# Alternating five convolution chunks with the z chunks of a mixer, and computing the convolution's Silu from a tanh and a product

## The reference, cut to what matters

```python
proj = u @ w_in
z, xbc, dt_raw, u5, g_a, g_b = jnp.split(proj, SPLITS, axis=-1)
# ssd branch
xbc = jax.nn.silu(causal_depthwise_conv(xbc, conv_w, conv_b))   # width 3072, 4 taps
xs, bm, cm = xbc[:2048], xbc[2048:2560], xbc[2560:3072]         # (on the last axis)
dt = softplus(dt_raw + dt_bias); a = -exp(a_log)
y = ssd_chunked(xs * dt, a * dt, bm, cm) + d_skip * xs
y = y * silu(z)
y_a = groupnorm(y) @ w_branch_a
# s5 branch
y_b = s5_branch(u5, ...) @ w_branch_b
merged = sigmoid(g_a) * y_a + sigmoid(g_b) * y_b
```

## Time and profile before

| | |
|---|---|
| median of 3 runs | 3229.38 us |
| range of the runs | 3227.72 to 3231.2 us |
| the profiled execution | 3236.26 us |
| span in its profile | 3234.4 us |
| mean granted TensorE clock | 0.953 of full speed |
| PE / DVE / ACT busy | 92% / 69% / 52% of the span |

### The profile page before, as it was taken

One profiled execution on the slowest core, in us unless ns is written; L12 is line 12 of the kernel. 1 busy time (PEld: TensorE's weight loads), 2 busy tenths in 40 slices (PEclk: granted clock), 3 DMA queues, 4 the chain that ended last, 5 costly groups with the idle time before them and its releaser, 6 DMA issues.

```text
span 3234.4 us, 55445 instructions
## 1 busy us (share of the span) xinstructions
PE 2979.0 (92%) x22709; PEld 2763.9 (85%) x22709; DVE 2232.5 (69%) x2614; ACT 1674.7 (52%) x1838; POOL 74.2 (2%) x68
## 2 busy tenths in 40 slices
PE   8988899989989889898989988988779999999997
PEld 7988898979989888888889987988579989999996
DVE  5778975655556779857555554555568888888887
ACT  4444566334444454563344444443456666666665
POOL 0000003000000000030000000000000000000000
PEclk9998999999999988999999998999889999999998
DMA  7553342446545533433555553545089999999996
GB/s 233 165 157 104 94 133 90 157 141 199 178 157 178 175 105 93 131 106 118 170 167 177 181 170 112 187 156 183 1 288 310 318 343 342 319 318 337 347 319 212
DMA packets 485886, 619.87 MB, mean 192 GB/s; under 512 B 31841, under 2 KB 436211, under 8 KB 485747
## 3 DMA queue, kind: packets, MB, share of 16 engines
q1 hardware_dynamic: 485747, 617.90, 58.3%
HBM read 616.81 MB, written 1.05 MB: 191 GB/s over the span
## 4 chain that ended last, share of the span: by engine, by line
PE 77%; DVE 13%; ACT 5%; issue 3%; DMA 1%; DVEq 0%; SPq 0%; ACTq 0%
PE PS L602 12%; PE PS L603 12%; PE PS L604 12%; PE PS L655 11%; PE PS L882 5%; PE PS L884 5%; PE PS L883 5%; DVE w_lo L1575 3%; PE PS L1064 3%; PE PS L1065 2%; PE PS L1066 2%; ACT w_hi L1139 2%; ACT w_hi L1506 1%; PE PS L1076 1%; PE PS L784 1%
## 5 line engine op out<-in xcount | busy, mean ns | idle before, releaser
L602 PE MATMUL PS<-x_hi,w_hi 128*128 128x256 f32 x3360 | 976.7, 291 | 13.1 <-DVE x_lo L2042 7.1
L603 PE MATMUL PS<-x_hi,w_lo 128*128 128x256 f32 x3360 | 967.2, 288 | 0.0
L604 PE MATMUL PS<-x_lo,w_hi 128*128 128x256 f32 x3360 | 966.1, 288 | 0.0
L1575 DVE TENSOR_TENSOR w_lo<-raw,w_hi 128x2048 fp32r<-128x2048 f32 x313 | 711.6, 2288 | 333.6 <-ACT w_hi L1139 332.9
L1139 ACT ACTIVATE w_hi<-raw 128x2048 fp32r<-128x2048 f32 x313 | 598.5, 1913 | 398.3 <-PE PS L655 249.1
L602 PEld LDWEIGHTS PS<-x_hi,w_hi 128*128 128x128 f32 x3360 | 662.9, 197 | 24.7 <-issue 12.0
L603 PEld LDWEIGHTS PS<-x_hi,w_lo 128*128 128x128 f32 x3360 | 663.0, 197 | 1.9
L604 PEld LDWEIGHTS PS<-x_lo,w_hi 128*128 128x128 f32 x3360 | 661.7, 197 | 0.0
L882 PE MATMUL PS<-w_hi,x_hi 128*128 128x256 f32 x1488 | 429.6, 289 | 8.4 <-DVE x_lo L2225 6.7
L884 PE MATMUL PS<-w_lo,x_hi 128*128 128x256 f32 x1488 | 421.8, 283 | 0.0
L883 PE MATMUL PS<-w_hi,x_lo 128*128 128x256 f32 x1488 | 421.7, 283 | 0.0
(11 more groups left out here) (393 smaller groups left out, 4098.0 us busy)
## 6 DMA issues: line engine op xcount, KB each, us to landing
raw<-in_w_gu_moe_dram SPq DMA_DIRECT2D x98, 1024.0 KB, 8.5
XC<-in_w_gu_moe_dram SPq DMA_DIRECT2D x80, 1024.0 KB, 9.6
raw<-in_w_in_dram SPq DMA_DIRECT2D x64, 1024.0 KB, 5.8
raw<-in_w_down_moe_dram SPq DMA_DIRECT2D x48, 1024.0 KB, 8.6
raw<-in_ffn_w_gate_dram SPq DMA_DIRECT2D x44, 1024.0 KB, 5.4
raw<-in_ffn_w_up_dram SPq DMA_DIRECT2D x44, 1024.0 KB, 6.7
raw<-in_ffn_w_down_dram SPq DMA_DIRECT2D x44, 1024.0 KB, 5.0
G<-in_w_down_moe_dram SPq DMA_DIRECT2D x40, 1024.0 KB, 9.5
```

The source lines that it names most:

```text
L602: mm(dst, w_hi[:, slot, w0:w0 + P], hi, start=start, stop=False, skip_group_check=True)
L603: mm(dst, w_lo[:, slot, w0:w0 + P], hi, start=False, stop=False, skip_group_check=True)
L604: return mm(dst, w_hi[:, slot, w0:w0 + P], lo, start=False, stop=True, skip_group_check=True)
L1575: tt(w_lo[:, slot, :], raw[:, slot, :], w_hi[:, slot, :].bitcast(F32), SUB)\
```

## The change

Two things are changed in both layers.

The order of the ticks: x(13) to x(19) stay (channels 8 to 11, 0, 1, 2). From tick 20 on z and x alternate, z(0), x3, z(1), x4, z(2), x5, z(3), x6, z(4), x7, and the last three are z(5), z(6), z(7). The first z tick is k = 20 instead of 25, and the work that was hung on it moves with it. The buffers of z change, since `conv_out` is now in use for longer.

The Silu of the convolution: `prm` holds the convolution's weights and biases times 0.5, so `conv_out` holds half the sum, ACT takes Tanh of it in tick k+2, and a new DVE instruction at the head of tick k+2 (`conv_silu`) forms (tanh + 1) * conv_out. To halve these columns the copy to `prm` is split in two. ACT's last tap of x(k) now waits for DVE's product of x(k-2). In the alternating ticks ACT also waits, ahead of the eviction of an x chunk, for DVE's `gate_z` of the tick before.

```diff
-TICKS = ... + [("x", i) for i in CONV_ORDER] + [("z", i) for i in range(8)]
+TICKS = [("u", i) for i in range(4)] + [("d", 0)] + [("g", i) for i in range(8)] + [("x", i) for i in CONV_ORDER[:7]] \
+    + [tick for i in range(5) for tick in (("z", i), ("x", i + 3))] + [("z", i) for i in (5, 6, 7)]
...
-        zbuf = [conv_out[:, 0], conv_out[:, 1], act_out[:, :, :]]
+        zbuf = [act_out[:, :, :], stage[:, :, :], wk(6912, 2, T)]
...
-                    fn(prm[:, :], PS[:, 7, 0:192], ACT.Copy).then_inc(s["prm_ready"], n.one("prm_ready"))
+                    fn(prm[:, 0:72], PS[:, 7, 0:72], ACT.Copy)
+                    fn(prm[:, 72:192], PS[:, 7, 72:192], ACT.Copy, scale=0.5).then_inc(s["prm_ready"], n.one("prm_ready"))
...
                 if i not in CONV_ORDER[:2]:
-                    act.wait_ge(s["silu_conv"], n.last("silu_conv"))
+                    act.wait_ge(s["silu_conv"], n.due("silu_conv"))
...
-                fn(XC[:, 2 * i:2 * i + 2, :], conv_out[:, i % 2, :, :], ACT.Silu)\
-                    .then_inc(s["silu_conv"], n.one("silu_conv"))
+                fn(XC[:, 2 * i:2 * i + 2, :], conv_out[:, i % 2, :, :], ACT.Tanh)\
+                    .then_inc(s["conv_tanh"], n.one("conv_tanh"))
...
                     if kind == "x":
+                        if z_at(k, 1) is not None:
+                            act.wait_ge(s["c_evicted"], n.due("c_evicted", k - ticks_seen))
+                            ticks_seen = k
                         last_tap(i)
...
+            def conv_silu(i):
+
+                dve.wait_ge(s["conv_tanh"], n.due("conv_tanh"))
+                x = XC[:, 2 * i:2 * i + 2, :]
+                stt(x, x, 1.0, conv_out[:, i % 2, :, :], ADD, MULT).then_inc(s["silu_conv"], n.one("silu_conv"))
...
                 for k, (kind, i) in enumerate(TICKS):
+                    if conv_at(k, 2) is not None:
+                        conv_silu(conv_at(k, 2))
...
-                    if k == 25:
+                    if k == Z_AT[0]:
                         dve.wait_ge(s["dtok_psum"], n.due("dtok_psum"))
...
+                    if z_at(k, 1) is not None:
+                        ssd_inputs(z_at(k, 1))
                     if kind == "z":
-                        if i >= 1:
-                            ssd_inputs(i - 1)
                         gate_z(i)
-                        if i >= 2:
-                            ssd_outputs(i - 2)
+                    if z_at(k, 1):
+                        ssd_outputs(z_at(k, 1) - 1)
```

More of the change, by code:

```diff
@@ L56 @@
 MIX = FFN1 + 3 * STEPS
-C_Z = MIX + 25
-C_A = C_Z + 8
+C_A = MIX + 33
 C_G = C_A + 8
@@ L214, with conv_at, z_at @@
 CONV_ORDER = [8, 9, 10, 11, 0, 1, 2, 3, 4, 5, 6, 7]
-TICKS = [("u", i) for i in range(4)] + [("d", 0)] + [("g", i) for i in range(8)] + [("x", i) for i in CONV_ORDER] \
-    + [("z", i) for i in range(8)]
-CONV_AT = [kind for kind, _ in TICKS].index("x")
+TICKS = [("u", i) for i in range(4)] + [("d", 0)] + [("g", i) for i in range(8)] + [("x", i) for i in CONV_ORDER[:7]] \
+    + [tick for i in range(5) for tick in (("z", i), ("x", i + 3))] + [("z", i) for i in (5, 6, 7)]
+X_AT = [TICKS.index(("x", i)) for i in CONV_ORDER]
+Z_AT = [TICKS.index(("z", i)) for i in range(8)]
+def conv_at(k, behind):
+    return CONV_ORDER[X_AT.index(k - behind)] if k - behind in X_AT else None
+def z_at(k, behind=0):
+    return Z_AT.index(k - behind) if k - behind in Z_AT else None
 S5_TILES = S5_PAIRS // 4
@@ L366, in build @@
                  "picked gathered scattered scatter_turned scatter_ready hidden_ready hidden_turned kh_ready y_copied sum_added mean_sum "
-                 "z_tanh moe_silu gate_odd up_odd down_odd gate_ready up_ready down_ready gate_used up_used down_used "
+                 "z_tanh conv_tanh moe_silu gate_odd up_odd down_odd gate_ready up_ready down_ready gate_used up_used down_used "
                  "act_step dve_step pool_step pool_waited sp_waited out_sent").split()
@@ L819, in mixer @@
                             part(t)
-                    if MIX + k == C_Z - 1:
+                    if k == Z_AT[0] - 1:
                         pe.wait_ge(s["e_read"], n.due("e_read"))
@@ L1269, in last_tap, with conv_tanh @@
                        scale=prm[:, 168 + t:169 + t], bias=prm[:, 72 + t:73 + t])
-            def silu_conv(i):
+            def conv_tanh(i):
                 act.wait_ge(s["tap_done"], n.due("tap_done"))
@@ L1309, in mixer @@
                 run[0] = 0
+                ticks_seen = 0
                 for k, (kind, i) in enumerate(TICKS):
@@ L1319, in mixer @@
                             part(t)
[L1320 to L1323, removed]
+                    if conv_at(k, 2) is not None:
+                        conv_tanh(conv_at(k, 2))
+                    if z_at(k, 1) is not None:
+                        ssd_decay(z_at(k, 1))
                     if kind == "z" and i >= 3:
@@ L1341, in mixer @@
                     if kind == "z":
-                        if i < 2:
-                            act.wait_ge(s["silu_conv"], n.last("silu_conv"))
                         wait_used(pos[0] + 1)
@@ L1349, in mixer @@
                 ssd_decay(7)
+                n.due("c_evicted", 33 + 8 - ticks_seen)
+                n.due("silu_conv", 2)
                 n.due("y_psum", 4)
@@ L1845, in s5_local, with evicted @@
                 dve.wait_ge(s["local_ready"], n.last("local_ready"))
-            def taps(i):
[L1849 to L1853, removed]
+            ticks_seen = [0]
+            def evicted(k):
+                if k >= ticks_seen[0]:
+                    dve.wait_ge(s["c_evicted"], n.due("c_evicted", k + 1 - ticks_seen[0]))
+                    ticks_seen[0] = k + 1
+            def conv_silu(i):
+                dve.wait_ge(s["conv_tanh"], n.due("conv_tanh"))
+                x = XC[:, 2 * i:2 * i + 2, :]
+                stt(x, x, 1.0, conv_out[:, i % 2, :, :], ADD, MULT).then_inc(s["silu_conv"], n.one("silu_conv"))
+            def taps(i):
+                evicted(X_AT[CONV_ORDER.index(i)])
                 for j in range(3):
@@ L1898, in gate_z @@
                 z = zbuf[i % 3]
-                stt(z, z, 1.0, PS[:, 4 + (C_Z + i - MIX) % 2, :].rearrange("p (u n) -> p u n", u=2), ADD, MULT)\
+                stt(z, z, 1.0, PS[:, 4 + Z_AT[i] % 2, :].rearrange("p (u n) -> p u n", u=2), ADD, MULT)\
                     .then_inc(s["c_evicted"], n.one("c_evicted"))
             def ssd_outputs(i):
-                dve.wait_ge(s["c_evicted"], n.due("c_evicted"))
+                evicted(Z_AT[i])
                 for u in range(2):
@@ L1939, in mixer @@
                 for k, (kind, i) in enumerate(TICKS):
+                    if conv_at(k, 2) is not None:
+                        conv_silu(conv_at(k, 2))
                     if k == 5:
-                        dve.wait_ge(s["c_evicted"], n.due("c_evicted", 5))
+                        evicted(4)
                         stt(dt_rows[:, 1, :], dt_rows[:, 0, :], -1.0, dt_rows[:, 0, :], MULT, MIN)\
@@ L1959, in mixer @@
                         s5_scan(t)
-                    if 0 <= k - CONV_AT - 1 < 12:
-                        taps(CONV_ORDER[k - CONV_AT - 1])
-                    if k == 25:
+                    if conv_at(k, 1) is not None:
+                        taps(conv_at(k, 1))
+                    if k == Z_AT[0]:
                         dve.wait_ge(s["dtok_psum"], n.due("dtok_psum"))
@@ L1975, in mixer @@
                 ssd_outputs(7)
-                n.due("silu_conv", 2)
+                n.due("c_evicted", 33 - ticks_seen[0])
+                ticks_seen[0] = 0
                 for i in range(8):
```

## The result

The changed kernel took 3242.87 us, the median of 13 runs (3235.49 to 3246.12), and the kernel before 3231.14 us in as many runs beside it (3227.72 to 3234.66). The ratio is 1.0035, with an interval of 1.0027 to 1.0042, so it is 11.7 us slower. The forecast was 3233.6 us, 4.2 us slower than the median of the first three runs, in a range of 3228 to 3240.

What follows compares the result with a forecast made beforehand. PE was taken as the bound, except DVE in ticks 15 and 16. Per layer 1.22 + 0.61 + 0.25 = 2.08 us, 4.2 for two, on the median of 3229.4 gave 3233.6 us, range 3228 to 3240.

Steps and rivals of the forecast that it cites:

- what bounds what: First layer's mixer: DVE bounds ticks 15 and 16, PE the stretches 412.6 to 466.0 and 474.1 to 540.1 us.
- the 12.8 us of the table loads: Rival: ten removed ACT table loads of 1.28 us were on the path, making the kernel faster, 3220.8 us; chance 0.04.
- only stalls could be won or lost: PE is already full, so only the dt_tok stall could be won: 1.6 us and 1.7 us of lost clock per layer.
- the products of ticks 15 and 16: DVE bounds these ticks, so two added products of 0.61 us come on the path: 1.22 us a layer, up to 1.6.
- the sign that the prediction named: Sign of being right: PE's wait for the S5 result at L737's successor grows from 4.8 to about 5.4 to 6.0 us.
- ticks 18 and 19: ACT's last tap waits for DVE's product of two ticks before, but is just not late: 0, up to 0.5 us.
- The closed chain: Last tap, w_hi, w_lo, product, next last tap: 6.2 us against a 5.76 us tick; would slow long runs of x ticks.
- the price of tick 20: First z tick: the product lengthens PE's dt_tok wait from 1.60 to 2.21 us: +0.61, up to 0.8 + 0.5.
- A clock under 0.7 after the dt_tok stall: One of the signs listed in advance that would show the prediction wrong.
- The rival on the clock: After the longer wait at the first z tick the clock falls deeper: 2.5 us more per layer, 3238.6 us; chance 0.17.
- the term for prm: Both layers' heads: splitting the prm copy in two costs +0.25 us each, between 0.1 and 0.36.

Runs made afterwards that it cites:

- no_product: The changed kernel, new tick order and tanh on ACT, without DVE's product, so it computes something else: 3229.71 us, 0.9994 of the kernel before.
- before_again: The kernel before, unchanged, run for a second profile: 3230.46 us.
- silu_only: The changed kernel with the old order of ticks, keeping the tanh on ACT and the product on DVE: 3246.26 us, 1.0047 of the kernel before.
- before_copy_later2: The kernel before with two idle DVE products ahead of the dt_tok copy, lengthening that wait in each layer: 3238.58 us, 1.0022 of the kernel before.
- after_copy_first: The changed kernel with DVE's dt_tok copy moved to the head of the first z tick, ahead of product and taps: 3229.24 us, 0.9994 of the kernel before.
- after_again: The changed kernel, unchanged, run for a second profile: 3242.57 us.

## Why the prediction was wrong

**Right: what bounds what.** PE is full through the alternating ticks at a clock of 1.00, no engine falls behind there, and the 12.8 us of the table loads did not come (no_product). The trace of before also settles what the earlier trace rows left open, whether ACT stands still behind a load: one load of tick 19 runs from 427.26 to 428.54 us, and the Silu behind it starts at 428.55. The reading that only stalls could be won or lost held; what a stall costs beyond its own length is the step that failed, below.

**Right in kind, too large in size: the products of ticks 15 and 16.** The term was 1.22 us a layer. In the second layer the two kernels start the mixer alike, at 1129.8 and 1130.1 us, and PE comes out of the dt_tok stall 1352.4 - 1130.1 = 222.3 us later, against 1378.9 - 28.8 (five ticks of 5.76) - 1129.8 = 220.3 before. The shift is 2.0 us, and 1.3 of it is the longer wait for dt_tok, so 0.7 us are left for the products of ticks 15 and 16, little more than half of the term. In the first layer it can't be read. The wait at L748 grew by 0.6 us, the sign that the prediction named, but the other wait for an S5 result, L738 (the old L727), shrank from 3.4 to 1.0 us, and in before_again L737 had 3.2 us. PE came out of the stall 219.7 us after the start of the mixer, against 220.2 and 218.6 in the two profiles of before.

**Partly wrong: ticks 18 and 19, "It is just not late: 0, up to 0.5."** For tick 19 it held in the first layer, and the wait is the forecast 2.2 us. (In tick 18 the last tap stood waiting for DVE's product in both layers, which the prediction did not see.) In the second layer it did not hold: ACT's last tap of tick 19 stood waiting for DVE's product and not for PE,

```profile
1343.08 1.02 ACT L1280 ACTIVATE conv_out<-PS,prm 128x256 f32<-128x256 f32 x2 [2.06 <-DVE XC L1876]
```

and the wait for dt_tok became 2.9 us. That is inside the bound that was given. The closed chain is real, 6.33 us a tick against the 6.2 that were worked out, and silu_only shows what the alternation protects from.

**Wrong: the price of tick 20, "+0.61".** This is the step that failed. It counted the longer wait as waiting alone, and put the loss of clock behind it at nothing more than before. The rows of before already had the clock at 0.74 after a 1.6 us wait, and the prediction used them only for a rival, with a chance of 0.17, that was to decide "once the wait is nearer to 4.8 than to 1.6". There is no such point near 3.2 us: 2.2 us of wait gave 0.57 to 0.72, as low as 5.4 and 5.8 us did (though 2.8 us left 0.86 once). before_copy_later2 measures the term alone: 2.4 us of wait cost 6.9 us. after_copy_first measures it from the other end: 5.1 us of wait were worth 13.6. "A clock under 0.7 after the dt_tok stall" was one of the prediction's own signs of being wrong, and it came in the first layer (0.57).

The mixers can be split where PE comes out of the stall. Ahead is the time from the mixer's start to there, behind from there to its end; of the kernel before, 28.8 us (its last five x ticks of 5.76) are moved from ahead to behind, where the changed kernel has these chunks:

| ahead + behind, us | first layer | second layer |
|---|---|---|
| before | 220.2 + 279.8 | 220.3 + 279.8 |
| before_again | 218.6 + 277.6 | 220.3 + 279.7 |
| after | 219.7 + 282.8 | 222.3 + 281.2 |
| after_again | 219.7 + 282.7 | 222.3 + 281.2 |

In the mean the change costs 1.1 us ahead, where the forecast had 1.83, and 2.8 us behind, where it had 0. The rival on the clock had put 2.5 us there: its size was right, and it was given a chance of 0.17.

**Too large: the term for prm.** From one root to the next at the head of the second layer the stretch grew by 0.06 us (4.44 to 4.50), not 0.25. Harmless.

**The sum now.** The mixer took 500.0, 500.1, 496.2 and 500.0 us in the two profiles of before, and 502.5, 503.5, 502.4 and 503.5 in those of after: 3.9 us a layer, 7.8 for both, where the forecast had 1.83 and 3.7. With the 3.4 us of the attention stretch it is 11.2 of the 11.7 us. The first feed-forward part, also untouched, was 1.7 us faster in the profiles of after (the spans of the profiles differ by some 9.6 us in the mean), so the account closes only to within such shifts, and how much of the 11.7 us is due to the attention in the mean of many runs stays open.

## What to carry to other kernels

Price a wait of TensorE together with what follows it: read the granted clock of the 10 us behind a comparable stall. Here 2.4 us of added wait cost 6.9 us (4.2 to 10.0), and 5.1 us of removed wait gave 13.6, so count some two to four times the length of a wait that grows from 1.6 to over 2 us. The same product cost nothing in the alternating ticks and most in front of a short signal which TensorE waits for (here a 0.3 us copy), and moving the signal ahead of independent work is an edit of a few lines. When work goes from one engine to another, write down the closed chain that the new wait makes between them and compare it with the tick: it was 6.33 us against 5.76. Where only two ticks in a row were of that kind it added 0 and 0.7 us to the wait, in the long run of silu_only 3.2 and 3.6. Before a gain of a few us is put down to an edit, look at the stretches that the edit does not touch: two of them changed by some 3 us each from one kernel to the next.

## What the runs showed of the hardware

The granted clock's pattern repeats to a good part: two profiles of the changed kernel agree to 0.01 in both layers behind the stall, and their mixers to 0.1 us. Of the kernel before, the second layer repeated and the first did not (0.86 and 500.0 us, then 1.00 and 496.2 us). A shift of 0.6 us in one place moved losses of 3.1 and 2.2 us away from two stretches of unchanged code, 145.7 to 142.6 and 156.9 to 154.7 us. A difference of 0.1% between two kernels can thus come from code that neither of them changed.

Clock already lost can be hidden as well: PE was busy 3.7 us more in the first layer's mixer (455.14 against 451.47 us) while the mixer grew by 2.5 us. PE's two waits for S5 results of DVE in ticks 15 to 17 were 1.8 us shorter in it (5.4 and 1.0 against 4.8 and 3.4 us), so what PE lost there was time in which it would have waited. The two rows by stretch, after and then before:

```profile
216.40:718.90 502.50, 455.14 (x4222) 427.86 (x4222) 379.42 (x509) 238.11 (x345) 37.84 (x32) 0.93 0.37 117
```

```profile
218.60:718.60 500.00, 451.47 (x4222) 424.88 (x4222) 366.02 (x497) 244.60 (x351) 37.01 (x32) 0.94 0.38 118
```
